# Expert search of a PEER block: comparisons written in one run, operands in PSUM, builds four to eight tiles earlier

## The reference

```
q  = (h @ w_query) as [T, 8 heads, 2, 64];   s = q . sub_keys -> [T, 8, 2, 128]
s_top, i_top = top_k(s, 16)                       # per head and half
cand = s_top[:,:,0,:,None] + s_top[:,:,1,None,:]  # 16 x 16 sums
best, bi = top_k(cand, 16);  ia, ib = bi // 16, bi % 16
e = i_top[0][ia] * 128 + i_top[1][ib]             # one of 16384 experts
g = softmax(best)
y = sum over the 128 slots of a token:  g * gelu(u[e] . x) * v[e]
```

## Time and profile before

| | |
|---|---|
| median of 3 runs | 1408.88 us (1406.36 to 1409.94) |
| the profiled execution, first to last instruction | 1406.0 us |
| TensorE busy | 1369.2 us, 97% |
| VectorE busy | 1198.2 us, 85% |
| ScalarE / GpSimd busy | 709.0 us, 50% / 775.0 us, 55% |
| HBM | 390.02 MB read, 47.22 MB written |

### The profile page before, as it was taken

How to read it: one execution, slowest core, us unless ns; L and a number is a source line. 1 busy time by engine, 2 the same in 40 slices (tenths; PEclk the granted TensorE clock), 3 DMA queues, 4 the chain that set the end, 5 groups by cost and what they waited for, 6 DMA issues and landing times.

```text
span 1406.0 us, 23810 instructions
## 1 busy us (share of the span) xinstructions
PE 1369.2 (97%) x8569; PEld 1267.3 (90%) x8569; DVE 1198.2 (85%) x2667; ACT 709.0 (50%) x1325; POOL 775.0 (55%) x465
## 2 busy tenths in 40 slices
PE   6999889999999999999999999999999999999999
PEld 2465556889999999999999999899999999999999
DVE  5767878677999889899998866599999989999997
ACT  1245874334436884488637853443434334443442
POOL 0000000104698877788787878676756668567660
PEclk9999999999999999999999999999999999999999
DMA  9830101565699999999999999999999999999996
GB/s 353 318 118 0 61 1 61 177 242 196 212 315 347 332 339 371 413 363 323 352 408 357 340 346 408 395 363 402 395 393 402 386 372 402 399 399 397 402 400 224
DMA packets 158230, 438.83 MB, mean 312 GB/s; under 512 B 16608, under 2 KB 50720, under 8 KB 156832
## 3 DMA queue, kind: packets, MB, share of 16 engines
q1 hardware_dynamic: 91632, 244.55, 47.5%
q0 software_dynamic: 46080, 167.79, 30.9%
q10 hardware_dynamic: 20400, 24.95, 5.0%
HBM read 390.02 MB, written 47.22 MB: 311 GB/s over the span
## 4 chain that ended last, share of the span: by engine, by line
PE 72%; DVE 12%; DMA 7%; issue 4%; ACT 2%; POOL 1%; SPq 1%; DVEq 0%; ACTq 0%
PE ps L1329 11%; PE ps L1331 11%; PE ps L1330 11%; PE ps L1380 6%; PE ps L1381 6%; PE ps L1382 6%; PE ps L1340 6%; PE ps L1023 5%; DVE y_tok L1894 4%; DMA raw<-in_v_tiles 3%; DVE lo L1881 2%; DMA act_in<-gelus 2%; DMA qkc<-in_w_ada 1%; DVE cf L1870 1%; PE ps L1181 1%
## 5 line engine op out<-in xcount | busy, mean ns | idle before, releaser
L866 ACT ACTIVATE hi<-raw 128x1024 fp32r<-128x1024 f32 x256 | 270.7, 1058 | 211.3 <-DMA raw<-in_v_tiles 139.8
L583 POOL TENSOR_TENSOR lo<-raw,hi 128x1024 fp32r<-128x1024 f32 x123 | 297.2, 2418 | 143.0 <-ACT hi L866 142.3
L1329 PE MATMUL ps<-h2hi,hi 128*128 128x352 f32 x1024 | 335.3, 327 | 2.9 <-POOL lo L583 2.9
L1331 PE MATMUL ps<-h2hi,lo 128*128 128x352 f32 x1024 | 330.5, 323 | 0.0
L1330 PE MATMUL ps<-h2lo,hi 128*128 128x352 f32 x1024 | 330.4, 323 | 0.0
L1380 PE MATMUL ps<-chi,hi 128*128 128x352 f32 x1008 | 324.3, 322 | 0.1
L1381 PE MATMUL ps<-clo,hi 128*128 128x352 f32 x1008 | 324.2, 322 | 0.0
L1382 PE MATMUL ps<-chi,lo 128*128 128x352 f32 x1008 | 324.2, 322 | 0.0
L596 POOL DMA_INDIRECT row_res<-in_v_tiles,E x91 | 175.3, 1927 | 103.9 <-DVE y_tok L1894 70.5
L1329 PEld LDWEIGHTS ps<-h2hi,hi 128*128 128x128 f32 x1024 | 193.0, 189 | 4.9 <-POOL lo L583 4.6
L1330 PEld LDWEIGHTS ps<-h2lo,hi 128*128 128x128 f32 x1024 | 192.7, 188 | 0.0
(11 more groups left out here) (311 smaller groups left out, 2161.9 us busy)
## 6 DMA issues: line engine op xcount, KB each, us to landing
raw<-in_u_tiles SPq DMA_DIRECT2D x128, 512.0 KB, 6.0
raw<-in_v_tiles SPq DMA_DIRECT2D x128, 512.0 KB, 7.8
gelus<-act_out ACTq DMA_DIRECT2D x128, 176.0 KB, 5.8
act_in<-gelus SPq DMA_DIRECT2D x128, 176.0 KB, 9.3
gates<-stage SPq DMA_DIRECT2D x32, 512.0 KB, 8.1
gate<-gates SPq DMA_DIRECT2D x32, 512.0 KB, 9.2
late<-in_w_ada SPq DMA_DIRECT2D x4, 2048.0 KB, 7.9
qkT<-in_w_ada SPq DMA_DIRECT2D x3, 2048.0 KB, 20.5
```

What stands on the lines that cost most here:

```text
L583: nc.gpsimd.tensor_tensor(lo[m % 3][:], raw[m % 3][:], hi[m % 3][:].bitcast(F32), ALU.subtract).then_inc(u_lo, 1)
L866: nc.scalar.activation(hi[m % 3][:], raw[m % 3][:], ACT.Copy).then_inc(t_hi, 1)
L1329: nc.tensor.matmul(out, hi[n % 3][:, cols], dense(h2hi, k), start=(k == 0), stop=False)
L1331: last = nc.tensor.matmul(out, lo[n % 3][:, cols], dense(h2hi, k), start=False, stop=(k == KD - 1))
```

## The change

- In `search` the comparisons write `eq` in one run of 256 elements each (`eq[:, j, :, :, :]`) instead of at a distance of 16, and the reduce reads it through a rearranged view.
- Small operands move between SBUF and PSUM: `sixf` and a copy of the first scores (`first_ps`), a copy of the second rank (`qr_ps`), the product of the shift (`past_ps`) and eR lie in PSUM, and `ab` (before: `abf`, PSUM) in SBUF. There are two copies more in a search, and a wait for `g_sb` of the build before.
- S0 is 9 instead of 11 and SEARCH 15 instead of 17: searches at tiles 9, 40, 71, builds at 24, 55, 86, `tail_at` 98. The steps of the rows in a search spread over SEARCH - 2 tiles.
- `own_low` goes: GpSimd makes all `lo` of the u tiles.
- The extra u rows have steps at four rows in three tiles, from tile 100 on, instead of two in a tile from tile 108 on; `more_at` stays 124.

```
-S0, SEARCH, BUILD, GP, GB = 11, 17, P // (2 * HB), 16, 4
+S0, SEARCH, BUILD, GP, GB = 9, 15, P // (2 * HB), 16, 4
...
-        (eq,), at_q = region(at_t, [("eq", [P, 2, PH, KTOP, KTOP], F32)])
+        (eq,), at_q = region(at_t, [("eq", [P, KTOP, 2, PH, KTOP], F32)])
...
-        abf = ps[:, 1, 0:2 * SLOTS].rearrange("p (a h k) -> p a h k", a=2, h=PH)
+        sixf = ps[:, 1, 0:2 * SLOTS].rearrange("p (a h k) -> p a h k", a=2, h=PH)
+        first_ps = ps[:, 2, 0:SLOTS].rearrange("p (h k) -> p h k", h=PH)
+        qr_ps, past_ps = (ps[:, 2, a * SLOTS:(a + 1) * SLOTS].rearrange("p (h k) -> p h k", h=PH) for a in (1, 2))
+        eR = ps[:, 2, 3 * SLOTS:3 * SLOTS + PH]
...
+        MORE_TILES = NT - 4 - (tail_at + 2)
...
-            row_step += [search_at[p] + 2 + j * PAUSES // FILL[p] for j in range(FILL[p])]
+            row_step += [search_at[p] + 2 + j * (SEARCH - 2) // FILL[p] for j in range(FILL[p])]
...
-        more_at = tail_at + 2 + (SU - SLOTS) // 2
-        row_step = row_step[:SLOTS] + [tail_at + 2 + j // 2 for j in range(SU - SLOTS)] + \
+        more_at = tail_at + 2 + MORE_TILES
+        row_step = row_step[:SLOTS] + [tail_at + 2 + j * MORE_TILES // (SU - SLOTS) for j in range(SU - SLOTS)] + \
...
-        own_low = [tail_at + 4 + 3 * j for j in range(5)]
...
-                if m not in own_low:
-                    low_u(m)
+                low_u(m)
...
                 if p >= 2:
                     dve.wait_ge(oh_used, group(p - 1, steps_of[p - 1], 0) + 2)
-                nc.vector.tensor_copy(sixf[:], six[:])
+                    dve.wait_ge(g_sb, group(p - 1, steps_of[p - 1], 0) + 2)
+                nc.vector.tensor_copy(sixf, six[:])
                 half = KTOP // 2
-                first, second = sv[:, 0, :, :], sv[:, 1, :, :]
+                second = sv[:, 1, :, :]
+                settled(nc.vector.tensor_copy(first_ps, sv[:, 0, :, :]))
...
-                settled(nc.vector.tensor_copy(qr[:], bia[:]))
+                nc.vector.tensor_copy(qr[:], bia[:])
+                settled(nc.vector.tensor_copy(qr_ps, bia[:, 1, :, :]))
                 pause()
...
-                settled(nc.vector.scalar_tensor_tensor(out=bia[:, 0, :, :].bitcast(F32), in0=qr[:, 0, :, :], scalar=float(half),
-                                                       in1=qr[:, 1, :, :], op0=ALU.is_ge, op1=ALU.mult))
-                tt_(abf[:, 0, :, :], qr[:, 0, :, :], bia[:, 0, :, :].bitcast(F32), ALU.add)
+                settled(nc.vector.scalar_tensor_tensor(out=past_ps, in0=qr[:, 0, :, :], scalar=float(half),
+                                                       in1=qr_ps, op0=ALU.is_ge, op1=ALU.mult))
+                tt_(ab[:, 0, :, :], qr[:, 0, :, :], past_ps, ALU.add)
...
-                        out=eq[:, :, :, :, j], in0=abf, scalar=float(j),
+                        out=eq[:, j, :, :, :], in0=ab[:], scalar=float(j),
...
-                settled(nc.vector.tensor_reduce(IJW[:, 0:2, :, :], eq[:], X, ALU.add))
+                settled(nc.vector.tensor_reduce(IJW[:, 0:2, :, :], eq[:].rearrange("p j a h k -> p a h k j"), X, ALU.add))
                 pause()
                 dve.wait_ge(best_exp, p + 1)
                 settled(nc.vector.tensor_reduce(eS[:], eW[:], X, ALU.add))
-                settled(nc.vector.reciprocal(eR[:], eS[:]))
+                settled(nc.vector.reciprocal(eR, eS[:]))
```

More of the change, by code:

```diff
@@ L147, in build @@
         (accs_late,), at_a = region(at_h, [("accs_late", [P, 2, CH], F32)])
-        (s, sv, six, sixf, best, bi, bia, qr, IJW, eW, eS, eR), at_t = region(at3, [
+        (s, sv, six, ab, best, bi, bia, qr, IJW, eW, eS), at_t = region(at3, [
             ("s", [P, 2 * PH, NK], F32), ("sv", [P, 2, PH, KTOP], F32), ("six", [P, 2, PH, KTOP], U32),
-            ("sixf", [P, 2, PH, KTOP], F32), ("best", [P, PH, KTOP], F32), ("bi", [P, PH, KTOP], U32),
+            ("ab", [P, 2, PH, KTOP], F32), ("best", [P, PH, KTOP], F32), ("bi", [P, PH, KTOP], U32),
             ("bia", [P, 2, PH, KTOP], U32), ("qr", [P, 2, PH, KTOP], F32), ("IJW", [P, 3, PH, KTOP], F32),
-            ("eW", [P, PH, KTOP], F32), ("eS", [P, PH], F32), ("eR", [P, PH], F32)])
-        (eq,), at_q = region(at_t, [("eq", [P, 2, PH, KTOP, KTOP], F32)])
+            ("eW", [P, PH, KTOP], F32), ("eS", [P, PH], F32)])
+        (eq,), at_q = region(at_t, [("eq", [P, KTOP, 2, PH, KTOP], F32)])
         (cand, eqI), at_t = region(at_t, [("cand", [P, PH, NC], F32), ("eqI", [P, 2, HB, P], F32)])
@@ L296, in build @@
         u_lo = sem("u_lo")
-        own_lo = sem("own_lo")
         v_lo = sem("v_lo")
@@ L478, in load_tile @@
                 if 3 <= m < NT + 3:
-                    sp.wait_ge(*low_done(m - 3))
+                    sp.wait_ge(u_lo, m - 2)
                 elif m >= NT + 3:
@@ L1323, in dot @@
             def dot(n):
-                pe.wait_ge(*low_done(n))
+                pe.wait_ge(u_lo, n + 1)
                 pe.wait_ge(gelu_done, n + 1)
@@ L1774, in search @@
                     dve.wait_ge(oh_used, group(p - 1, steps_of[p - 1], 0) + 2)
-                nc.vector.tensor_copy(sixf[:], six[:])
+                    dve.wait_ge(g_sb, group(p - 1, steps_of[p - 1], 0) + 2)
+                nc.vector.tensor_copy(sixf, six[:])
                 half = KTOP // 2
-                first, second = sv[:, 0, :, :], sv[:, 1, :, :]
+                second = sv[:, 1, :, :]
+                settled(nc.vector.tensor_copy(first_ps, sv[:, 0, :, :]))
                 tt_(cand[:, :, 0:half * KTOP].rearrange("p h (i j) -> p h i j", j=KTOP),
-                    first[:, :, 0:half].unsqueeze(3).to_broadcast([P, PH, half, KTOP]),
+                    first_ps[:, :, 0:half].unsqueeze(3).to_broadcast([P, PH, half, KTOP]),
                     second.unsqueeze(2).to_broadcast([P, PH, half, KTOP]), ALU.add)
-                settled(tt_(cand[:, :, half * KTOP:NC], first[:, :, half:KTOP], second[:, :, 0:1].to_broadcast([P, PH, half]), ALU.add))
+                settled(tt_(cand[:, :, half * KTOP:NC], first_ps[:, :, half:KTOP], second[:, :, 0:1].to_broadcast([P, PH, half]), ALU.add))
                 top16(lambda a: best[:, a, :], lambda a: bi[:, a, :], lambda a: cand[:, a, :], PH, pause)
@@ L1804, in search @@
                 settled(nc.vector.tensor_reduce(eS[:], eW[:], X, ALU.add))
-                settled(nc.vector.reciprocal(eR[:], eS[:]))
+                settled(nc.vector.reciprocal(eR, eS[:]))
                 pause()
                 out = wg[:, 0:SLOTS].rearrange("p (h k) -> p h k", h=PH) if p == 0 else IJW[:, 2, :, :]
-                return tt_(out, eW[:], eR[:].unsqueeze(2).to_broadcast([P, PH, KTOP]), ALU.mult)
+                return tt_(out, eW[:], eR.unsqueeze(2).to_broadcast([P, PH, KTOP]), ALU.mult)
             def one_hot(p, i, half):
@@ L1900, in _ @@
             for g in range(SLOTS, SU):
-                m = tail_at + 3 + (g - SLOTS) // 2
-                if (g - SLOTS) % 2 == 0 and m in own_low:
-                    dve.wait_ge(t_hi, m + 1)
-                    tt_(lo[m % 3][:], raw[m % 3][:], hi[m % 3][:].bitcast(F32), ALU.subtract).then_inc(own_lo, 1)
                 row_dot(g)
```

5 lines of the change are left out of this document (1 added, 4 removed).

## The result

| | before | changed kernel |
|---|---|---|
| median of 4 runs | 1409.41 us (1406.36 to 1410.91) | 1442.54 us (1440.6 to 1446.25) |
| profiled execution, first to last instruction | 1406.0 us | 1442.4 us |
| granted clock, mean | 0.996 | 0.987 |

The ratio is 1.0228 (95% interval 1.0207 to 1.025): slower, as forecast, but by 33 us and not by 10, and 15.5 us above the range.

The account below looks back on a forecast made before the run. From 325 us on TensorE was taken as the bound. Standstills of 5.4 + 4.8 + 4.8 at builds 1 to 3, less 4.5 at the end of the u tiles, gave +10.5 on the median 1408.88: 1419.4 us, range 1416 to 1427.

Parts of the forecast that it names:

- stop ahead of build 1: TensorE at L1347 waits for VectorE's search 1: 5.4 us, at least 4.8 by the Exp, 7.5 or 9.3 in worse cases.
- stops ahead of builds 2, 3: TensorE waits at IJW's transposes because the Exp now follows the gelu of the last tile before the build: 4.8 us each.
- wait for gates inside builds 2, 3: A build's first copy to `stage` waits for 16 gate transfers; they were to land in time, cost 0.
- end of the u tiles: GpSimd makes all `lo` and issues 4 gathers in 3 tiles; TensorE's wait for `lo` goes: -4.5 us (0 to -4.6).
- the Exp ends last: In searches 2 and 3 the Exp ends 60.7 us after the search's start; VectorE could start eS at 58.6.
- The cast: Cast of `six` in search 1, with PSUM as target: 2.46 to 0.30 us, -2.2 (from 0 to -2.2).
- the comparisons: The 16 comparisons in search 1: 0.466 to 0.35 us each, -1.8 us (from 0 to -2.7).
- the gathered row that no longer waits: Search 1's wait for its first gathered row, 3.7 us, goes because gathers may start at tile 12 instead of 14.
- the standstill itself hides them: Gates land in 8.1 us, the first copy to `stage` comes 9.6 us after the search's end: cost 0.
- ready at 430.9: Search 1 starts at 376.4 and takes 54.5 us instead of 61.7, so ends at 430.9; TensorE arrives at 425.6.
- rival (a): Strided reduce costs double, +4.4 us; standstill of build 1 becomes 12, with the others 17, so 1426; chance 0.15.
- VectorE's savings are worth nothing: In searches 2 and 3 the Exp ends after VectorE is ready, so VectorE's some 6 us saved win nothing.

Follow-up runs that it names:

- the Exp: Changed kernel with the Exp of searches 1 to 3 behind the gelu of tile search_at+12 instead of +14: 1444.13 us, ratio 1.0262.
- the pace: Changed kernel with the row steps of a search spread over 15 tiles as before, instead of 13: 1435.62 us, ratio 1.0197.
- the run with the later scores: Changed kernel with the key scores of search 3 loaded at tile build_at+6 instead of build_at+3: 1438.42 us, ratio 1.0205.
- the experiment on it: Changed kernel with 60, 24 and 24 unused products on TensorE ahead of the transposes of builds 1, 2 and 3: 1444.81 us, ratio 1.0229.
- the rows of search 1: Changed kernel with later scores, Exp at +12, row steps over 15 tiles, plus rows shared 5, 12, 12 instead of 9, 10, 10: 1430.43 us, ratio 1.0154.
- the schedule alone: Kernel before with only S0, SEARCH, row_step, own_low and more_at of the changed one, search operations as before: 1439.77 us, ratio 1.0208.
- scores, Exp and pace: Changed kernel with scores loaded at build_at+6, Exp at search_at+12 and row steps over 15 tiles: 1428.83 us, ratio 1.0137.
- Exp and pace: Changed kernel with the Exp at search_at+12 and row steps over 15 tiles: 1431.14 us, ratio 1.0174.

## Why the prediction was right and where it was wrong

| term of the sum | forecast, us | profile, us |
|---|---|---|
| stop ahead of build 1 | 5.4 | 11.8 |
| stops ahead of builds 2, 3 | 4.8 + 4.8 | 4.74 + 4.74 |
| wait for gates inside builds 2, 3 | 0 | 6.64 + 2.62 |
| half clock after the five stops | no term | about 9.4 (half of 18.8) |
| end of the u tiles | -4.5 | -3.1 |
| sum | +10.5 | +36.8; the spans differ by 36.4 |

Stops are measured here from start to start of the products around them, less what a product takes.

**Right.** "the Exp ends last" in searches 2 and 3: eS is released by ScalarE's eW, and both stops are 4.74. The working was right to 0.1 us, with the Exp 2.46 after the gelu's start (587.68 to 590.14; 2.47 forecast) and the last product at 0.28. The cast (0.42, with 0.30 forecast), the comparisons (0.34) and the gathered row that no longer waits came about as forecast too. The two copies took 0.28 and 0.29. The end of the u tiles gave 3.1 of the 4.5 us; four waits for `lo` of at most 0.4 us were left. Right was also the sign, at 0.90. The Trainium skill, "ScalarE: Activation LUTs", What ACT_TABLE_LOAD costs, has 1380 ns of drain with a load of 1283; here the load takes 1.28, ScalarE was idle 0.39 ahead of it, and the Exp starts 0.02 behind it (588.53, 589.83), so no such drain is in this trace.

**Wrong, first: "the standstill itself hides them. Without it they would be next."** This step failed. It took the landing time of before (8.1) and the sending of before, one gate transfer each 3.84 us. Both changed: the last gates were sent at 596.01, 3.8 us after TensorE had come back, and took 10.7. The sending hangs on `lo`, this on GpSimd's queue, that on a gather, and that on VectorE's next row; by the pace `SEARCH - 2` a gather is in the queue during the reduce, and that reduce is 3 us longer. Putting the pace back took the wait to zero (1.64 us of ScalarE's idle time remain) with the stops at L1343 unchanged; loading the scores later took 4.8 us of it in build 2. The prediction counted the transfers and not what they stand behind. With the old pace its sentence held: the stop hid the gates, and when the Exp made that stop shorter they were next, with 6.38 us in build 2.

**Wrong, second: search 1, "ready at 430.9".** It was ready at 437.7. Three errors add to this: the search started at 379.08 and not at 376.4 (+2.7), since the reduce of search 0 ended at 376.33, after the Exp (374.83), and the expert numbers, beside `lo` again, took 1.15 and not 0.30; the reduce of search 1 took 7.03 and not 4.42 (+2.6); and the product eW at L1781, two operands in SBUF with GpSimd's `lo` beside it, took 2.33 where before it took 0.69 (+1.6). 430.9 + 6.9 = 437.8. (In the run with the later scores this product took 0.29, and the next instruction, also from SBUF to SBUF, 2.42 in its place.) This is rival (a), with the price that it named (12 against 11.8), at a chance of 0.15. That the two agree so closely is partly luck: its "+4.4" was 2.6, and the 1.6 of the product is not in it. The working took 0 for an operation that no row showed, though it held the row that spoke against it: scattered writes cost 0.11 each. The Trainium skill, "SBUF — State Buffer", in its specifications on cachelines, says that accesses which keep crossing to new lines pay; the runs agree (7.03 against 4.42 for the reduce of search 1 with nothing but the layout of `eq` changed). The page gives no figure for it.

**Wrong, third: no price for the clock.** Five stops, each with a fall to 1.2 GHz that outlasts it, 9 us by the rows. The rows of before could not show it, as TensorE never stopped there so long. That products start 0.29 us apart and not 0.16 is measured; what a version without the falls would take is not, since the experiment on it only moved the first one.

**Wrong, in a claim that did not count.** VectorE was to be idle for 7 to 8 us ahead of eS in searches 2 and 3; it was 2.22. VectorE could have started eS 58.56 us after the search began (529.38 to 587.94), exactly as before the change. Some 6 us were to be saved; the strided reduce used 3.2 of that, and L1783, from SBUF to SBUF, took 2.43 us beside a `lo` instead of 0.21. Nothing hung on it, but the reserve on which "VectorE's savings are worth nothing" rested was far smaller.

**Where the expected gain of each cure went.** Measured one at a time on their own waits, the Exp takes away 4.2 us of stops, the pace 9.3 and the rows of search 1 6.4: 20 us. Together, and with the scores, they gave 12 on the median, although the stops of builds 2 and 3 grew when rows were moved there. The last gates of a build are sent at the load of tile search_at + 19, about when TensorE reaches the next build, and took 7.5 to 12.9 us in these combinations, with the DMA engines full in the search (share 1.01, and 1.02 before the change). Before the change the first copy to `stage` came 5.3 us after the transposes (596.78 to 602.11). So in these runs with 15 tiles the build stops until those gates have landed once the stop ahead of it is short.

## What to carry to other kernels

When a stage is shortened, list everything that has to be over by its end (the instruction moved by tile number, the transfers sent one per tile, and the queue that each of them stands in), and work out the arrival of each; they stand one behind another, so the price is that of the last and curing one gives back only the distance to the next. Do not take a landing time or a sending rhythm from the old schedule if the engine that paces it is edited. An operation with a layout that no row shows is priced by the nearest row that has such a layout, not at nothing.

## What the runs showed of the hardware

- A reduce of 4096 fp32 elements takes 4.42 us if neighbours are side by side, and 7.0 to 7.6 us if they are 1 KB apart; a comparison that writes 256 elements at a distance of 64 bytes takes 0.60 to 0.62 us, and 0.41 if it writes them in one run.
- Beside GpSimd's `lo` a product of 128 elements with two SBUF operands took 2.33 us (416.89), and one with an operand in PSUM 0.28 (437.39); a cast of 256 took 2.46 from SBUF to SBUF (404.92, before the change) and 0.43 to PSUM (347.90). Without `lo` beside them the SBUF forms took 0.29 both (440.15 before the change, 554.98 with the schedule alone), so the move of the cast to PSUM costs 0.13 us where no `lo` is in its way.
- After stops of 2.6 to 11.8 us TensorE worked 2.9 to 5.6 us at 1.2 GHz, its products 0.29 us apart instead of 0.16. Of the short stops, those of 2.36 and 1.86 us (scores, Exp and pace) had no fall behind them, and one of 2.0 (Exp and pace, 748 us) had one from 749.6 us on. With idle products through the stop the clock held, and then fell at the return to full work.
- The same transfer of 512 KB landed in 5.2 to 12.9 us. With the 1 MB of scores issued just ahead the last one took 10.7 us, and 7.2 without; the rest of the spread was not traced.
